# The short convolution of the recurrent branch, done by GpSimd in place of VectorE

## The reference, cut to what matters

```python
xc = causal_depthwise_conv(xr, conv_w[l], conv_b[l])   # y[s] = b + sum_k w[k] * x[s - 3 + k], k = 0..3, per channel
r = sigmoid(blockdiag(xc, w_gate_a) + b_a)
i = sigmoid(blockdiag(xc, w_gate_x) + b_x)
a = exp(-8 * r * softplus(-lru_lambda))
h[s] = a[s] * h[s-1] + sqrt(1 - a[s]**2) * (i[s] * xc[s])
```

## Time and profile before

| | us |
|---|---|
| three runs | 2721.28, 2723.76, 2724.84 |
| median | 2723.76 |
| the profiled execution | 2725.73 |
| its span, first to last instruction | 2723.9 |
| PE / DVE / ACT / POOL busy | 2637.8 / 1724.4 / 1342.5 / 57.8 |
| mean granted clock of PE | 0.983 |

### The profile page before, as it was taken

The page is one execution under the profiler, slowest core; times in us unless marked ns, Lnnn a source line. Parts: engine busy times, 40 slices in busy tenths (PEclk is TensorE's granted clock), DMA queues, the critical chain, the costliest instruction groups (busy, mean ns, idle before and its releaser), DMA issues.

```text
span 2723.9 us, 38217 instructions
## 1 busy us (share of the span) xinstructions
PE 2637.8 (97%) x14934; PEld 2259.6 (83%) x14934; DVE 1724.4 (63%) x1902; ACT 1342.5 (49%) x1551; POOL 57.8 (2%) x28
## 2 busy tenths in 40 slices
PE   7899998999999999999999999999999999999998
PEld 6688886888788988888888788888878888898887
DVE  6665576655766656666666666666656666665665
ACT  5444454444644545454454544544545454454543
POOL 0000000000000000000000000000000000000000
PEclk9799997999999999999999999999999999999999
DMA  7145541555455435545543455555325555543451
GB/s 287 58 175 187 187 180 61 181 189 189 161 195 185 155 109 189 195 172 200 186 170 124 151 189 185 186 185 185 109 101 192 193 177 194 186 161 118 172 194 66
DMA packets 63399, 454.62 MB, mean 167 GB/s; under 512 B 7088, under 2 KB 7344, under 8 KB 8768
## 3 DMA queue, kind: packets, MB, share of 16 engines
q1 hardware_dynamic: 61920, 448.82, 45.9%
q0 software_dynamic: 944, 3.18, 0.3%
q10 hardware_dynamic: 432, 1.14, 0.1%
HBM read 452.06 MB, written 1.05 MB: 166 GB/s over the span
## 4 chain that ended last, share of the span: by engine, by line
PE 89%; DVE 5%; ACT 4%; issue 1%; DMA 1%; SPq 0%; DVEq 0%; ACTq 0%
PE tb L480 23%; PE tb L478 13%; PE acc L265 10%; PE acc L266 9%; PE acc L267 9%; PE tb L477 3%; DVE w_lo L207 2%; PE acc L234 2%; PE acc L236 2%; PE acc L237 2%; ACT w_hi L200 1%; PE acc L808 1%; PE tb L296 1%; PE acc L809 1%; PE acc L810 1%
## 5 line engine op out<-in xcount | busy, mean ns | idle before, releaser
L207 DVE TENSOR_TENSOR w_lo<-raw,w_hi 128x2048 fp32r<-128x2048 f32 x417 | 956.0, 2295 | 354.2 <-ACT w_hi L200 353.4
L200 ACT ACTIVATE w_hi<-raw 128x2048 fp32r<-128x2048 f32 x426 | 814.2, 1913 | 364.8 <-PE acc L267 297.3
L480 PE MATMUL tb<-xT,w_hi 128*128 128x512 f32 x2772 | 987.8, 396 | 0.0
L478 PE MATMUL tb<-xT,w_lo 128*128 128x256 f32 x3168 | 818.4, 279 | 0.0
L478 PEld LDWEIGHTS tb<-xT,w_lo 128*128 128x128 f32 x3168 | 597.0, 188 | 33.8
L480 PEld LDWEIGHTS tb<-xT,w_hi 128*128 128x128 f32 x2772 | 520.1, 188 | 107.1
L265 PE MATMUL acc<-w_hi,cat 128*128 128x512 f32 x1024 | 403.1, 394 | 6.7 <-issue 3.5
L266 PE MATMUL acc<-w_hi,cat 128*128 128x512 f32 x1024 | 399.9, 391 | 0.0
L267 PE MATMUL acc<-w_lo,cat 128*128 128x512 f32 x1024 | 399.8, 390 | 0.0
L265 PEld LDWEIGHTS acc<-w_hi,cat 128*128 128x128 f32 x1024 | 193.1, 189 | 47.0 <-issue 4.2
L267 PEld LDWEIGHTS acc<-w_lo,cat 128*128 128x128 f32 x1024 | 193.1, 189 | 41.0
(11 more groups left out here) (337 smaller groups left out, 3266.0 us busy)
## 6 DMA issues: line engine op xcount, KB each, us to landing
raw<-in_stream SPq DMA_DIRECT2D x426, 1024.0 KB, 4.8
h<-in_x SPq DMA_DIRECT2D x2, 512.0 KB, 4.8
gain<-in_gains POOLq DMA_DIRECT2D x2, 512.0 KB, 9.7
xn<-in_gates POOLq DMA_DIRECT2D x2, 512.0 KB, 9.0
out<-xn SPq DMA_DIRECT2D x2, 512.0 KB, 2.7
cst<-in_consts ACTq DMA_DIRECT2D x1, 960.5 KB, 12.2
big<-in_pT POOLq DMA_DIRECT2D x2, 256.0 KB, 5.4
big<-in_lam_qk POOLq DMA_DIRECT2D x1, 256.0 KB, 11.4
```

The source lines that it names most:

```text
L200: act.activation(w_hi[:, k % SPLIT, :], raw[:, k % RAW, :], ACT.Copy).then_inc(hi_done, 1)
L207: dve.tensor_tensor(w_lo[:, k % SPLIT, :], raw[:, k % RAW, :], w_hi[:, k % SPLIT, :], ALU.subtract).then_inc(lo_done, 1)
L478: last = pe.matmul(banks[f][:, 0:SEQ], lo, xT[:, kt, 0, :], start=False, stop=False)
L480: last = pe.matmul(banks[f], hi, both, start=False, stop=kt == KT - 1)
```

## The change

DVE no longer does the convolution. POOL does it, in a new function `conv_pool`, called in POOL's list right behind the issue of the gate weights. POOL has no fused multiply-add here: a tile's first tap stays one multiply-add with two scalars, and each of the other three taps becomes a multiplication into a temporary (slices of `a_r` or `a_i`, free at that time) and an addition, with a wait on POOL's own semaphore between them. PE still waits for `conv` of tile 3.

```diff
+        def conv_pool(pool, l):
+
+            par = lru_par[:, l, :]
+            for t in range(4):
+                pool.wait_ge(*when("a_taken", (l, t // 2)))
+                for k_ in range(4):
+                    src = a_x[:, t, k_:k_ + SEQ]
+                    w = par[:, L_CONV + 4 * k_ + t:L_CONV + 4 * k_ + t + 1]
+                    if k_ == 0:
+                        ins = pool.tensor_scalar(a_xc[:, t, :], src, w, par[:, L_CONVB + t:L_CONVB + t + 1], ALU.mult, ALU.add)
+                    else:
+                        term = a_r[:, k_, :] if t % 2 == 0 else a_i[:, k_, :]
+                        if t >= 2:
+                            pool.wait_ge(*when("conv", (l, t - 2)))
+                        pool.tensor_scalar(term, src, w, None, ALU.mult).then_inc(*sig("own_pool", ("term", l, t, k_)))
+                        pool.wait_ge(*when("own_pool", ("term", l, t, k_)))
+                        ins = pool.tensor_tensor(a_xc[:, t, :], term, a_xc[:, t, :], ALU.add)
+                    ins.then_inc(*(sig("conv", (l, t)) if k_ == 3 else sig("own_pool", ("cv", l, t, k_))))
+
         def mix_a_dve(dve, l, c, n):
...
             for j in range(2):
                 take(j)
-            par = lru_par[:, l, :]
-            for t in range(4):
-                if t % 2 == 0:
-                    dve.wait_ge(*when("a_taken", (l, t // 2)))
-                for k_ in range(4):
-                    src = a_x[:, t, k_:k_ + SEQ]
-                    w = par[:, L_CONV + 4 * k_ + t:L_CONV + 4 * k_ + t + 1]
-                    if k_ == 0:
-                        ins = dve.tensor_scalar(a_xc[:, t, :], src, w, par[:, L_CONVB + t:L_CONVB + t + 1], ALU.mult, ALU.add)
-                    else:
-                        dve.wait_ge(*when("own", ("cv", l, t, k_ - 1)))
-                        ins = dve.scalar_tensor_tensor(a_xc[:, t, :], src, w, a_xc[:, t, :], ALU.mult, ALU.add)
-                    ins.then_inc(*(sig("conv", (l, t)) if k_ == 3 else sig("own", ("cv", l, t, k_))))
             for j in range(2, 6):
                 take(j)
...
                     pool.dma_start(a_bd, gates[l, :, :]).then_inc(*sig("gates_in", l, 16))
+                    if l == 0:
+                        pool.wait_ge(*when("start_in", 0))
+                    conv_pool(pool, l)
```

## The result

| | median us | runs | ratio to before |
|---|---|---|---|
| before | 2722.52 | 2719.28 to 2724.84 | |
| changed | 2752.39 | 2752.26 to 2753.72 | 1.0112 [1.0097, 1.0128] |

The change costs 30 us (1.1%), against 22 us predicted. It is slower, as forecast, and within the range (2733 to 2766). The profiled executions differ by 26.8 us (2752.49 against 2725.73).

A forecast was written before the change was run, and what follows sets the result against it. PE was taken to bound the kernel, busy 97% of the span. Two layers of 9.0 us later gates and 2.0 us of clock gave 22.0 us: 2747.7 against the profiled execution, 2746 as median; range 2733 to 2766.

The forecast's parts named there:

- The path: At PE's gates: a late `conv` is paid in full, 9.0 us a layer; POOL alone would finish before group 5 ends.
- The exclusion: POOL beside DVE's splits: each split with two SBUF inputs shuts POOL out for 2.25 us, six a layer.
- The mis-sized term: POOL's multiplications: 16 a layer at 500 ns each, 8.0 us (6.2 to 11.6), within 17.9 us of POOL work.
- rival 2: POOL's multiplications are slower than its additions, 1.1 us each: delay 18.6 us a layer, total 2765; chance 15%.
- my signs of being wrong: POOL not stretched beside splits, a multiplication over 0.75 us (wait over 13 us), or PE idle under 5 us before the gates.
- The clock: At the gates: after some 10 us idle PE's clock falls to 1.2 GHz, costing some 2.0 us a layer.
- Rival 3: PE's clock stays low behind the gates: 2.5 us more a layer, total 2751; chance 15%.
- The gain: PE's waits for the split before group 5 go: at most 1.39 + 0.57 = 2.0 us.
- Rival 5: Setting up POOL's first arithmetic delays the convolution: layer 0 costs 6 us more, total 2752; chance 4%.
- Rival 1: The convolution fits under PE's column groups and the time is not slower: -2.0 us, 2722; chance 7%.
- Rival 4: Partial sharing with the splits or quick multiplications (15 us of work), no clock loss: 2736 or down to 2729; chance 11%.

The follow-up runs named there:

- experiment 3: Changed kernel with five splits a layer subtracting PSUM (`acc`) instead of `w_hi`, so the output is wrong: 2724.12 us, ratio to before 1.0000.
- 6: Changed kernel with POOL doing only tiles 0 and 1, with two-operation multiplications, and DVE tiles 2 and 3 behind `take(2)`: 2718.53 us, ratio to before 0.9976.
- experiment 1: Changed kernel with a second operation, + 0.0, on layer 0's multiplications and layer 1's taps in reversed order: 2753.6 us in one run.
- experiment 2: Changed kernel with 100 extra matmuls on PE between group 5 and its wait for the convolution: 2746.65 us, ratio to before 1.0078.
- 7: Kernel before, POOL doing nothing, with DVE's `take(2)` and its split ahead of the convolution instead of behind it: 2723.16 us, ratio to before 0.9993.
- 9: Unedited repeat of 6, half of the convolution on POOL: 2718.60 us, ratio to before 0.9974.
- 10: Unedited repeat of 7, only DVE's order changed against the kernel before: 2719.12 us, ratio to before 0.9984.
- 5: Changed kernel with an added 0.0 as second operation of all of POOL's multiplications, in both layers: 2747.45 us, ratio to before 1.0080.
- experiment 8: Unedited repeat of the changed kernel: 2752.46 us, ratio to before 1.0104.

## Why the prediction was right, and where it was off

- **The path.** PE's wait for `conv` decides, it is paid in full (28.0 us found at the gates, 26.8 between the profiles), and POOL alone would nearly have fitted: shown by experiment 3 (same operations, ratio 1.0000) and by 6, where POOL takes part, is done in time and costs nothing. The six splits of layer 0 started within 0.1 us of the forecast, counted from `take(0)`.
- **The exclusion.** Read from one place in the trace before (a split of 3.90 us beside a copy), it carried over to multiplications and additions. Experiment 3 takes the second SBUF operand from five of the six splits, which keep their starts and their length, and 11.2 us of POOL's busy time a layer vanish. The rule of the Trainium skill, "SBUF — State Buffer", "Who interferes with whom", is borne out in both of its parts: two SBUF inputs exclude, one does not. I charged 6 x 2.25 = 13.5 us; it took 11.5 (34.3 - 22.8). The six splits lasted 14.1 us. In 1.6 of them the POOL operation under way got through first, and each operation that stood needed some 0.15 us less than its own length once the split was through.
- **The mis-sized term.** I took 0.50 us for a multiplication, next to the copy's rate. The multiply-add was 0.55, but the 12 single multiplications took 0.92, outside my bounds of 0.385 and 0.725. So rival 2 came true in kind, at less than its 1.1. POOL's own work was 22.8 us instead of 17.9. These 4.9 us, less the 2.0 of the point above, are the 2.9 us by which each layer is later than forecast (11.9 on average against 9.0): 5.8 us of the difference between 28 and 22. The bounds were wrong in kind: they followed the number of operands, and experiment 1 shows that the form of the instruction counts.
- **Signs and luck.** One of my signs of being wrong came true, a multiplication of over 0.75 us, and with it a wait of 13.5 us in layer 0 where I had said 9 to 11 (12.3 in layer 1). The total came out as near as it did partly by luck: 9.8 us too little for POOL's work in both layers met 4.0 too much for the exclusion.
- **The clock.** 2.0 us a layer were charged, 2.4 and 1.6 were found (experiment 2). Rival 3, a clock low behind the gates as well, did not happen: L265 follows 0.54 us behind the sigmoids and its successors take 0.28 us, as before.
- **The gain.** Both waits before group 5 went, 2.0 us, and were no gain while `conv` was late. Experiments 6, 7, 9 and 10 are rid of them without the cost, though only 0.9 us of the 2.0 reaches the gates in their profiles.
- **Rival 5**, a late first operation: POOL's first multiply-add took 0.55 us like the others, 0.2 us behind `take(0)`. It did not happen.
- **Rival 1**, that the convolution fits, asked for at most 20.9 us of work and no shutting out. Neither held (22.8 and 11.5 us). It is the shutting out that made the kernel slower: without it POOL ends 2 us behind group 5 (59.1) and the time is that of before (experiment 3).
- **Rival 4**, sharing in part: 2.5 of the 14.1 us were shared, but the work was 22.8 us and not 15.

## What to carry to other kernels

Before work moves to GpSimd, count the time in which VectorE reads two operands from SBUF in the same stretch. Nearly all of it is taken from GpSimd (here 11.5 of 14.1 us), so an engine that looks idle has less time to give than it seems. Measure the very form of the instruction that is to move, not its neighbour with as many operands. And look first whether the wait that the move would end (here 2 us) goes away by changing the order on the engine that has the work; here that was worth 0.16% in one set of runs and was not told from nothing in the other.

## What had not been expected of the hardware

- On GpSimd a `tensor_scalar` of 128x256 float32 with one operation took 0.92 us and with two operations 0.48 (second scalar a constant) or 0.55 (both scalars for each channel). Adding 0.0 as second operation nearly halves the time (experiments 1 and 5). Why is not shown.
- The exclusion leaves a little room at the end of a GpSimd operation. Splits that began within one, in the changed kernel and in experiments 1, 5 and 6, were longer by what it had left less 0.14 us (left 0.64: 2.79 us instead of 2.29; 0.58: 2.72; 0.31: 2.46; 0.28: 2.42). Only the single multiplications differ: with 0.64 us left the split took 2.34, with 0.55 left 2.29. So the 0.44 us by which they are slower than the two-operation form do not hold VectorE up.
- Executions of one kernel spread over 5 to 15 us, five to twelve at a time (2711 to 2726 in experiments 9 and 10). The short ones have the higher mean granted clock: in 9 the two of 2711.41 us had 0.988 and 0.989, the one of 2725.56 had 0.982; in 10 it was 0.988 at 2711.18 and 0.981 at 2726.18. A profile can show where. Experiments 6 and 9 are the same kernel. Behind the same pause of 1.45 us the matmuls slowed down from 0.28 to 0.41 us in 6 and did not in 9:

```profile
421.17 0.46 PE L744 MATMUL tb<-big 64*128 64x128 f32 x2 [1.45 <-ACT big L1723]
...
424.33 0.41 PE L234 MATMUL acc<-xT,w_hi 128*128 128x256 f32 x1
```

```profile
426.48 0.46 PE L744 MATMUL tb<-big 64*128 64x128 f32 x2 [1.45 <-ACT big L1723]
...
429.57 0.28 PE L234 MATMUL acc<-xT,w_hi 128*128 128x256 f32 x1
```

  The first two rows are of 6, the others of 9. A wait of 12 or 13 us let the clock fall in both profiles of the changed kernel (gates of 6.09 and 5.33 us, and of 6.14 and 5.37 in experiment 8).
